# Alternating the row halves in the state-query products, and moving the second layer's third modulation group to its output projection and the transition behind it

## What is computed

```python
mod_lat = jnp.split((jax.nn.silu(c) @ w_mod[i] + b_mod[i])[:, None, :], N_MOD, axis=-1)
h_lat = modulate(rmsnorm(x, g_mix_pre[i]), mod_lat[0], mod_lat[1])
y_lat, _, _ = token_mixer(h_lat, *mix_w, s_f, s_b)
x = x + mod_lat[2] * rmsnorm(y_lat, g_mix_post[i])
x = ffn_sublayer(x, mod_lat[3], mod_lat[4], mod_lat[5], g_ffn_pre[i], ...)
...
o_intra = jnp.einsum('bnhij,bnjhv->bnihv', scores, v)
o_inter = jnp.einsum('bnihd,nbhdv->bnihv', q * jnp.exp(g), s_start)
```

## Time and profile before

| | us |
|---|---|
| median of three runs | 1793.74 |
| lowest to highest | 1792.3 to 1801.79 |
| the profiled execution | 1791.2 |
| its span in the trace | 1789.4 |
| PE busy in the span | 1684.3 (94%) |
| DVE, ACT, POOL busy | 665.7, 516.7, 572.5 |

### The profile page before, as it was taken

One profiled execution on the slowest core, in us unless ns is written; L12 is line 12 of the kernel. 1 busy time (PEld: TensorE's weight loads), 2 busy tenths in 40 slices (PEclk: granted clock), 3 DMA queues, 4 the chain that ended last, 5 costly groups with the idle time before them and its releaser, 6 DMA issues.

```text
span 1789.4 us, 22456 instructions
## 1 busy us (share of the span) xinstructions
PE 1684.3 (94%) x9084; PEld 1353.3 (76%) x9084; DVE 665.7 (37%) x847; ACT 516.7 (29%) x752; POOL 572.5 (32%) x259
## 2 busy tenths in 40 slices
PE   5799999999899999999999988999998899999995
PEld 1577877877578888888888856778786588888884
DVE  1510236558832111111112696115647521122136
ACT  3533213422432211221122245242322422222220
POOL 0522222115332222232232443233304444444433
PEclk9899999999999999999999999999989999999998
DMA  8434342124521122122112374342213133333221
GB/s 329 167 117 143 118 142 96 46 94 153 188 67 63 59 62 69 59 59 71 59 59 70 94 259 143 118 141 72 82 49 105 47 97 96 100 95 94 94 97 67
DMA packets 47867, 185.18 MB, mean 103 GB/s; under 512 B 4854, under 2 KB 8822, under 8 KB 41144
## 3 DMA queue, kind: packets, MB, share of 16 engines
q1 hardware_dynamic: 40816, 168.48, 28.2%
q10 hardware_dynamic: 6984, 15.75, 2.4%
HBM read 175.83 MB, written 8.39 MB: 103 GB/s over the span
## 4 chain that ended last, share of the span: by engine, by line
PE 72%; issue 12%; DVE 9%; POOL 3%; ACT 3%; DMA 1%; ACTq 0%; DVEq 0%; POOLq 0%
PE A L617 61%; POOL w_lo L572 2%; PE A L785 2%; DVE x L1309 2%; DVE y L1316 2%; PE A L781 1%; DVE y L1308 1%; PE N L849 1%; DVE h_lo L1321 1%; DMA posc<-pos_col 1%; PE G L756 1%; DVE sqb L1283 1%; PE N L769 1%; PE A L792 1%; PE A L749 1%
## 5 line engine op out<-in xcount | busy, mean ns | idle before, releaser
L572 POOL TENSOR_TENSOR w_lo<-raw,w_hi 128x1024 fp32r<-128x1024 f32 (+1 forms) x219 | 525.0, 2398 | 1111.6 <-ACT w_hi L873 1111.6
L617 PE MATMUL A<-h_hi,w_hi 128*128 128x512 f32 (+1 forms) x1808 | 570.2, 363 | 33.7 <-DVE h_lo L1321 22.5
L617 PE MATMUL A<-h_lo,w_hi 128*128 128x512 f32 (+1 forms) x1808 | 558.6, 356 | 0.0
L617 PE MATMUL A<-h_hi,w_lo 128*128 128x512 f32 (+1 forms) x1808 | 557.6, 356 | 0.0
L873 ACT ACTIVATE w_hi<-raw 128x1024 fp32r<-128x1024 f32 (+1 forms) x219 | 228.1, 1042 | 811.8 <-PE A L617 773.4
L617 PEld LDWEIGHTS A<-h_hi,w_hi 128*128 128x128 f32 x1808 | 306.2, 190 | 111.5 <-issue 19.8
L617 PEld LDWEIGHTS A<-h_lo,w_hi 128*128 128x128 f32 x1808 | 307.9, 191 | 49.4 <-issue 0.2
L617 PEld LDWEIGHTS A<-h_hi,w_lo 128*128 128x128 f32 x1808 | 306.4, 190 | 51.3
L1293 DVE TENSOR_TENSOR sqb<-sqb,A 128x768 f32<-128x768 f32 (+1 forms) x44 | 36.1, 821 | 427.0 <-PE A L617 426.7
L617 PE MATMUL A<-g_hi,w_hi 128*128 128x512 f32 (+1 forms) x528 | 169.5, 360 | 0.5 <-DVE g_lo L1296 0.4
L617 PE MATMUL A<-g_lo,w_hi 128*128 128x512 f32 (+1 forms) x528 | 168.0, 357 | 0.0
(11 more groups left out here) (131 smaller groups left out, 1219.9 us busy)
## 6 DMA issues: line engine op xcount, KB each, us to landing
raw<-stream SPq DMA_DIRECT2D x219, 512.0 KB, 3.5
mraw<-modw SPq DMA_DIRECT2D x42, 1024.0 KB, 4.9
raw<-modw SPq DMA_DIRECT2D x6, 1024.0 KB, 15.0
x<-x_keep ACTq DMA_DIRECT2D x4, 1536.0 KB, 8.0
x_keep<-x ACTq DMA_DIRECT2D x4, 1024.0 KB, 7.2
x<-xT SPq DMA_DIRECT2D x1, 2048.0 KB, 9.5
x_keep<-x ACTq DMA_DIRECT2D x4, 512.0 KB, 6.2
out_dram<-x ACTq DMA_DIRECT2D x4, 512.0 KB, 2.8
```

The costliest lines, as they stand in the source:

```text
L572: pool.tensor_tensor(w_lo[:, n % RING, 0:WIDTH[n]], raw[:, n % RAW, 0:WIDTH[n]], w_hi[:, n % RING, 0:WIDTH[n]].bitcast(F32), ALU.subtract) ...
L617: m = pe.matmul(dst[:, t0:t1], a, b[:, k, t0:t1], start=(first and p == 0), stop=(last and p == 2))
```

## The change

First, in `o`, PE does for each pair pr the four products of L781 of both heads, then the eight state-query products with hp innermost, so that consecutive ones lie in different row halves. Numbers and operands of the products stay.

Second, the third modulation group of layer 1 leaves the input projection. Four pieces stand ahead of `wout`, two behind `mean`, one behind the second and one behind the fourth `sq`, `mturn` ahead of `rstd`. The group is summed in G0 in place of N.

```diff
-MOD_UNIT = {(0, 0): "G0", (0, 1): "N0", (0, 2): "N0", (1, 0): "G0", (1, 1): "G0", (1, 2): "N0"}
+MOD_UNIT = {(0, 0): "G0", (0, 1): "N0", (0, 2): "N0", (1, 0): "G0", (1, 1): "G0", (1, 2): "G0"}
...
             order.append(("mean", L, w, 0))
+            if more:
+                modk(1, 2, (4, 5))
             steps("res", 0, range(KT))
             if more:
-                steps("sq", 0, range(KT))
+                for k in range(KT):
+                    steps("sq", 0, (k,))
+                    if k in (1, 3):
+                        modk(1, 2, (6 + k // 2,))
+                order.append(("mturn", 1, 2))
                 order.append(("rstd",) + nxt + (0,))
...
-            if 3 <= x < 3 + KT:
-                modk(L, 1 if L == 0 else 2, (x - 3,))
-            if x == 3 + KT:
-                order.append(("mturn", L, 1 if L == 0 else 2))
+            if L == 0 and 3 <= x < 3 + KT:
+                modk(L, 1, (x - 3,))
+            if L == 0 and x == 3 + KT:
+                order.append(("mturn", L, 1))
...
         order.append(("msq", L, tiles[-1]))
+        if L == 1:
+            modk(1, 2, range(4))
         order.append(("wout", L))
...
-                    for h in range(HEADS):
-                        pr, hp = divmod(h, 2)
-                        row = slice(hp * 64, hp * 64 + 64)
+                    for pr in range(2):
                         for g in range(2):
-                            pe.matmul(o_at(b, h), vtok[:, tt, h * DV:(h + 1) * DV], Pm[:, b, hp, g, pr, :],
-                                      start=(g == 0), stop=False)
+                            for hp in range(2):
+                                h = 2 * pr + hp
+                                pe.matmul(o_at(b, h), vtok[:, tt, h * DV:(h + 1) * DV], Pm[:, b, hp, g, pr, :],
+                                          start=(g == 0), stop=False)
                         for g in range(2):
                             for c in range(2):
-                                m = pe.matmul(o_at(b, h)[:, c * 64:c * 64 + 64], S[row, g, 2 * tt + c, pr, :],
-                                              E[row, b, g, 2, pr, c * 64:c * 64 + 64], start=False, stop=(g == 1 and c == 1))
+                                for hp in range(2):
+                                    row = slice(hp * 64, hp * 64 + 64)
+                                    m = pe.matmul(o_at(b, 2 * pr + hp)[:, c * 64:c * 64 + 64], S[row, g, 2 * tt + c, pr, :],
+                                                  E[row, b, g, 2, pr, c * 64:c * 64 + 64], start=False,
+                                                  stop=(g == 1 and c == 1))
```

## The result

The changed kernel takes 1768.68 us (median, 1768.12 to 1772.21); the kernel before, run beside it, 1797.76 us (1792.3 to 1802.07). The ratio is 0.9854, with a 95% interval of 0.9825 to 0.9884: 1.5% faster. The kernel before lies at one of two levels, 17 of its 31 timed runs at 1791.9 to 1793.7 us and 14 at 1800.7 to 1804.3 us, and so does the kernel with the moved group alone, while none of the 40 runs of the kernels with reordered products shows a second level; what makes it stays open. The profiled executions, 1791.2 and 1768.12 us, have spans of 1789.4 and 1766.3 us, 23.1 us apart; the medians are 29.1 us apart, since the profiled execution of the kernel before is as short as the shortest of its timed runs. I account for the 23.1 us that the traces show.

What follows compares the result with a forecast made beforehand. TensorE, busy in 94% of the span, was taken to bound the kernel. Terms -22 - 8.9 + 10 + 1.5 = -19.4 us gave 1771.8 from the profiled execution, 1774.3 from the median; named 1773, range 1760 to 1786.

Steps and rivals of the forecast that it cites:

- State-query products: In the `o` tiles, alternating row halves run side by side: 2.2 us less per tile, 22 us in ten tiles.
- the first of my two readings: In `o`, sixteen state-query instructions cost what eight cost now, 1.04 us; with L781's saving, 2.5 us less per tile.
- rival E: Better: last tile of layer 1 ends before the clock falls, halves run at 110 ns, pieces cost 7: 1764, 18%.
- The drain: In `o`, changing from full array to halves and back costs about 0.16 us; eight changes per tile become four.
- Input projection: In layer 1, taking out the modulation pieces and their transposes saves 8.9 us of TensorE, ends 8.0 and 9.5.
- The pieces ahead of the output projection: Ahead of layer 1's `wout`, four pieces, later ones waiting for buffers and at half clock, lose 10 us, ends 6.5 and 14.
- SP stopped: Four pieces in a row hold back `wout`'s sixth chunk on SP's queue, but TensorE does not wait for it.
- The transition: Behind layer 1's mean, ACT's copy to `mrow` waits for piece 7 and delays the squares: 1.5 us lost, ends 0 and 4.
- A: In `o`, weight loads of the two halves stay in series, so ten tiles gain only 10 us: 1785, 8%.
- B: In `o`, alternation gives nothing because the halves drain at each turn; only the moves count: 1793, 5%.
- C: Slower: thinner tiles let the clock fall earlier, a tile of 8 us costing 16; 1822 if in six tiles, 4%.
- D: Dearer pieces: 2 and 3 land late, `wout` starts 14 us behind the mean, piece 7 holds ACT 4 us: 1780, 15%.

## Why the prediction was right, point by point

Forecast 1773 us in a range of 1760 to 1786, faster by over 0.5%; measured 1768.68. The sum was -19.4 us; the traces are 23.1 us apart, and the medians 29.1, of which the 6 us beyond the traces had no term in the prediction. The mechanism held at each place but the transition, where its share stays open. The largest miss of a term is that of the products, 2.4 us. That the rest came so near is in part luck: 4 us of clock that the sum did not hold were won in the tiles, 1.8 us were lost in stretches without an edit, and 1 us ahead of the tiles.

- **State-query products**, predicted -22. Measured -27.4 over the two tile stretches. Per tile it was 2.44 us and not the 2.2 that I took: the first of my two readings, a group of 16 at 1.04 us and L789 at 1.09, held to 0.01 us. The pace of the score products was the wrong row to lean to, since each of those streams twice as many columns, as the prediction itself noted. That is 24.4 us in ten tiles. Another 3.4 us are the half clock of the kernel before's last tile, which stood in rival E; it is gone with the move alone too, so it can't be put down to the alternation. 0.7 us more is of the same kind: behind layer 0's last tile the clock of the kernel before reads 0.54 in 378 to 381, that of the changed kernel 1.00. About 1 us went the other way ahead of layer 0's tiles.
- **What is late next**: DVE was to stay free while a tile shrank by no more than 2.8 us. It shrank by 2.44 and TensorE is busy for all 7.79 us.
- **The drain.** That a turn from the full array to halves and back costs about 0.35 us together, and that fewer turns gain, is shown by four turns in place of two (7.0 us in twenty extra turns). The two gains add as in the first reading: alternation alone 1.76 us per tile, the turns 0.68, both 2.44. Larger groups alone give 1.45 and not 0.68, since two groups of one half each, one behind the other, already overlap at their meeting.
- **Input projection**, predicted -8.9. Measured -8.7.
- **The pieces ahead of the output projection**, predicted +10. Measured +9.0: start at 10.4 us behind the last mean for 10.5, end at 55.4 for 56.4. The term for the half clock was 2 us and came out near 1: the 192 products take 44.91 us, and 43.77 with the clock at 1.00 in the kernel with two pieces ahead of the last tile. Two pieces ahead of the last tile show that the cause is the two buffers.
- **SP stopped** by four pieces in a row: no wait for stream chunks in the projection, as worked out; its 192 products take 44.91 us.
- **The transition**, predicted +1.5. Measured +2.3. The step named, ACT's copy behind piece 7, is in the trace: the fifth square comes 2.4 us later than before. I had put the step at 1.1 us for all squares together; behind the copy, squares seven and eight wait again, for TensorE (0.76 and 0.23 us), which the prediction did not have. But taking the wait for the copy away did not shorten the transition, so its share stays open. The kernel with two pieces in the transition, both right behind the mean, has a transition 1.5 us shorter than that with four; whether that is the number of pieces or their place is not shown.
- **The rivals.** A and B fall by the groups' length: sixteen in 1.04 us. C, the clock falling in the tiles, did not come: it reads 1.00 in all ten. D did not come: the output projection starts at 10.4 us and not 14. Of E, the pace of the halves and the last tile at full clock came; that the pieces cost 7 us did not.

## What to carry to other kernels

Where products use half of the array's rows, put the two halves beside each other and keep products of the full array out from between them; here sixteen instructions then took 1.04 us, as long as eight before. Work moved into idle time brings its own waits: a piece behind a two-buffer load is only free if its transfer lies under something, so start the first pair one stage earlier. And look at each engine's queue where a moved step lands: `mturn` ahead of the residual on DVE made the transition 0.9 us longer than behind it. And look at the clock in the stretches without an edit before you explain the last few microseconds: here it moved up to 3.4 us in a stretch.

## What the runs showed of the hardware that I had not expected

TensorE does not hold to program order between row halves: a matmul of the free half started 110 ns ahead of three earlier ones of the busy half, and eight instructions of one half behind eight of the other took 1.53 us rather than 1.92. And the clock differs from trace to trace in a stretch without an edit: the same last tile took 9.11 us at full clock with the group moved and 12.56 at 0.67 before, though the products in it are the same and only the work ahead of it differs.
